# A two-layer hybrid attention encoder step: five places in the hand-written order of its engines

## What is computed

```python
z = x @ W_in                    # four head groups and a gate of width 2048
# A: forgetting attention, 4 heads   B: chunk band with relative bias, 4 heads
# C: sliding window, 4 query and 2 kv heads, rotary, sinks
# D: attention into 256 memory tokens, 4 heads, keys and values = mem @ W_mem_kv
y = (concat(heads) * silu(gate)) @ W_out
x = LayerNorm(ALPHA * x + y)
```

## Time and profile before

| | |
|---|---|
| median of the timed runs | 1963.86 us (1961.84 to 1964.38) |
| the profiled execution | 1964.82 us, span 1962.9 us, mean granted clock 0.994 |
| busy | PE 1914.5 us (98%), DVE 1395.5 (71%), ACT 872.5 (44%), POOL 153.6 (8%) |
| chain that ended last | PE 89%, DVE 3%, DMA 3%, ACT 2% |

### The profile page before, as it was taken

One profiled execution on the slowest core, in us unless ns is written; L12 is line 12 of the kernel. 1 busy time (PEld: TensorE's weight loads), 2 busy tenths in 40 slices (PEclk: granted clock), 3 DMA queues, 4 the chain that ended last, 5 costly groups with the idle time before them and its releaser, 6 DMA issues.

```text
span 1962.9 us, 37789 instructions
## 1 busy us (share of the span) xinstructions
PE 1914.5 (98%) x15232; PEld 1888.9 (96%) x15232; DVE 1395.5 (71%) x2435; ACT 872.5 (44%) x1557; POOL 153.6 (8%) x280
## 2 busy tenths in 40 slices
PE   7999999999999999999999999999999999999996
PEld 6999999999999999999999999999999999989996
DVE  6976676666677674777888666666677667657776
ACT  6543333333444444544574333333344444444444
POOL 0011010000000001000001000000000000100000
PEclk9999999999999999999999999999999999999998
DMA  8533333333222224555664323323323222335563
GB/s 302 210 108 108 118 121 101 121 121 121 100 94 98 102 90 176 192 206 195 224 224 142 117 97 106 110 103 115 114 94 119 76 88 104 126 136 205 192 216 144
DMA packets 71622, 271.70 MB, mean 138 GB/s; under 512 B 10108, under 2 KB 19964, under 8 KB 59664
## 3 DMA queue, kind: packets, MB, share of 16 engines
q1 hardware_dynamic: 44720, 202.13, 29.4%
q0 software_dynamic: 16320, 53.21, 7.6%
q10 hardware_dynamic: 10432, 14.29, 2.0%
HBM read 236.71 MB, written 35.50 MB: 139 GB/s over the span
## 4 chain that ended last, share of the span: by engine, by line
PE 89%; DVE 3%; DMA 3%; ACT 2%; issue 1%; POOL 0%; SPq 0%; ACTq 0%; DVEq 0%
PE GB L702 54%; PE GB L613 16%; PE GB L559 3%; PE AB L642 3%; PE AB L684 3%; PE GB L936 3%; DMA WR<-in_wt 2%; PE AB L653 2%; PE GB L574 1%; ACT S L1026 1%; DMA o_rest<-BD 1%; ACT WH L997 1%; DVE WL L1509 1%; PE AB L689 0%; DVE XL L2092 0%
## 5 line engine op out<-in xcount | busy, mean ns | idle before, releaser
L702 PE MATMUL GB<-XH,WH 128*128 128x272 f32 x2112 | 614.8, 291 | 0.0
L702 PE MATMUL GB<-XH,WL 128*128 128x272 f32 x2112 | 608.9, 288 | 0.0
L702 PE MATMUL GB<-XL,WH 128*128 128x272 f32 x2112 | 608.8, 288 | 0.0
L1069 ACT CAST WH<-WR 128x512 fp32r<-128x512 f32 (+1 forms) x336 | 249.1, 743 | 433.8 <-PE GB L702 219.9
L702 PEld LDWEIGHTS GB<-XH,WH 128*128 128x128 f32 x2112 | 398.3, 189 | 1.9
L702 PEld LDWEIGHTS GB<-XH,WL 128*128 128x128 f32 x2112 | 398.3, 189 | 0.0
L702 PEld LDWEIGHTS GB<-XL,WH 128*128 128x128 f32 x2112 | 397.3, 188 | 0.0
L1653 DVE TENSOR_TENSOR WL<-WR,WH 128x512 fp32r<-128x512 f32 (+1 forms) x336 | 281.2, 838 | 64.1 <-ACT WH L1069 59.8
L997 ACT CAST WH<-WR 128x2048 fp32r<-128x2048 f32 x88 | 167.9, 1908 | 207.5 <-PE GB L613 149.5
L1509 DVE TENSOR_TENSOR WL<-WR,WH 128x2048 fp32r<-128x2048 f32 x88 | 201.6, 2290 | 52.7 <-ACT WH L997 52.4
L702 PE MATMUL GB<-TH,WH 128*128 128x272 f32 x576 | 166.6, 289 | 0.0
(11 more groups left out here) (280 smaller groups left out, 2891.6 us busy)
## 6 DMA issues: line engine op xcount, KB each, us to landing
WR<-in_wt SPq DMA_DIRECT2D x192, 512.0 KB, 4.1
WR<-in_wt SPq DMA_DIRECT2D x88, 1024.0 KB, 4.8
XR<-out POOLq DMA_DIRECT2D x64, 136.0 KB, 2.8
out<-OY ACTq DMA_DIRECT2D x24, 272.0 KB, 2.2
OY<-o_rest POOLq DMA_DIRECT2D x2, 2992.0 KB, 14.4
out<-OY ACTq DMA_DIRECT2D x8, 544.0 KB, 5.0
out<-KT POOLq DMA_DIRECT2D x16, 272.0 KB, 3.5
out<-VT POOLq DMA_DIRECT2D x16, 272.0 KB, 3.6
```

Of the source, the lines that this page charges most:

```text
L702: mm = pe.matmul(out, w[:, k, :], x[:, k, :], start=(start and k == 0 and i == 0), stop=(stop and k == chunks - 1 and i == 2))
L1069: act.copy(weight_block(name)[0], weight_source(p, name)).then_inc(b_hi, 1)
```

## The change

It edits five places. (1) `DVE_PLAN[0]`: ("mv", 7) goes ahead of ("w", 6). (2) Late heads on ACT: `scale_probs` moves ahead of d1, and in d and e ahead of `mem_key`. (3) Pair b: the scores move from behind p7 to behind p6 (the hook name changes with the place). (4) `last_head`: `exps(MEM, u + 3)` goes ahead of the waits for `zh` and `ld_o`, all eight casts follow it, and DVE's `invert_sums` goes ahead of all `o_lo`. (5) `first_out_tiles`: chunk 15 of s = 0 runs between the second and third pass of s = 1, and the mean goes ahead of chunk 15 of s = 1.

```diff
@@ DVE_PLAN[0]
-     ("w", 6), ("mv", 7), ("w", 7), ("tokens", 0)],
+     ("mv", 7), ("w", 6), ("w", 7), ("tokens", 0)],
@@ first_out_tiles
+                def last_chunk(s):
+                    for i, (w, x) in passes:
+                        mm = part(s, [KC - 1], i, w, x, False, i == 2)
+                    mm.then_inc(zd, 1)
...
+                        if s == 1 and i == 2:
+                            last_chunk(0)
                         part(s, range(KC - 1), i, w, x, i == 0, False)
                     if s == 0:
                         between()
-                for s in range(2):
-                    for i, (w, x) in passes:
-                        mm = part(s, [KC - 1], i, w, x, False, i == 2)
-                    mm.then_inc(zd, 1)
                 mean()
+                last_chunk(1)
@@ two_tiles (TensorE); late_head asks for "p6" in pair b
                 sum_product("p7", "s3", 1)
-                hook("p7")
                 pe.wait_ge(c_copy, copied(p, "p1"))
                 sum_product("p6", "s2", 2)
+                hook("p6")
@@ late_head (ScalarE), pair a
                     exps(MEM, u - 1)
-                next_blocks(a, "d1")
-                if j:
                     scale_probs(MEM, u - 1, t - 1)
-                next_blocks(a, "a12")
+                next_blocks(a, "d1", "a12")
@@ pair d
                 exps(SWA, u + 1)
+                scale_probs(SWA, u + 1, t + 1)
                 mem_key(u + 2, kl + 1, dm)
                 if j == 0:
                     next_blocks(d, "d1")
-                scale_probs(SWA, u + 1, t + 1)
@@ pair e
                 exps(MEM, u + 2)
+                scale_probs(MEM, u + 2, t + 2)
                 mem_key(u + 3, kl + 2, dm + 1)
-                next_blocks(e, "d1")
-                scale_probs(MEM, u + 2, t + 2)
-                next_blocks(e, "a12")
+                next_blocks(e, "d1", "a12")
@@ last_head (ScalarE)
                 take_o(u + 2, KC - 2)
+                exps(MEM, u + 3)
                 act.wait_ge(zh, l + 1)
                 act.wait_ge(ld_o, 32 * (l + 1))
-                for c in range(4):
-                    o_hi(c, 0)
-                exps(MEM, u + 3)
-                for c in range(4, 8):
+                for c in range(8):
                     o_hi(c, 0)
                 scale_probs(MEM, u + 3, t + 3)
@@ last_head (VectorE)
                 soft_in(MEM, u + 3)
-                for c in range(8):
-                    o_lo(c, 0, l)
                 invert_sums(u + 3)
-                for c in range(8, KC - 1):
+                for c in range(KC - 1):
                     o_lo(c, 0, l)
```

More of the change, by code:

```diff
@@ L823, in late_head @@
                     mix(MEM, u - 1, kl - 1, dm=dm - 1)
-                two_tiles(l, late_pair(l, j, 1), {"p7": lambda: late_scores(SWA, l, u, kl, q)})
+                two_tiles(l, late_pair(l, j, 1), {"p6": lambda: late_scores(SWA, l, u, kl, q)})
                 two_tiles(l, late_pair(l, j, 2), {"p2": own_probs, "p5": lambda: mix(SWA, u, kl, vu)})
```

## The result

The changed kernel takes 1942.57 us, the median of four runs (1940.90 to 1943.88), beside 1964.12 for four runs of the kernel before (1961.84 to 1966.39): ratio 0.989, 95% interval 0.9873 to 0.9907. The profiled execution took 1940.90 us (span 1939.0, mean granted clock 0.996), 23.9 less than that of before. The forecast was 1941.0, range 1937.5 to 1949.5.

A forecast was written before the change was run, and what follows sets the result against it. PE is busy 98% of the span, so only its waits and clock falls can go: 10.4 + 0.7 + 2.05 + 2.95 + 3.0 + 1.2 + 3.0 = 23.3 us off 1964.82 gives 1941.5, taken as 1941.0; range 1937.5 to 1949.5.

The forecast's parts named there:

- Edit 2, 10.4 us: Late heads: scaling probabilities earlier on ACT removes six waits of PE's transposes, 10.4 us over both layers.
- cover of `mix`: Pair d: DVE's copies of transposed probabilities end about 1.5 us before PE reaches `mix`.
- rival B: Late heads: the wait moves from transposes to `mix`, losing about half the scaling gain; 1946 us, chance 0.11.
- rival D: Late heads: ACT holds d1 and key casts behind scaling that waits for a late reciprocal; slower, 1989 us, chance 0.03.
- Edit 3, 0.7: Pair b, j = 0, layer 0: p6's matmuls cover the scores' wait, gaining 0.7 us; nothing taken as lost elsewhere.
- Edit 4, 2.05 and 2.95: Last head: earlier exponentials bring chunk 8's cast forward, ending PE's pass 2.05 us earlier in layer 0, 2.95 in layer 1.
- Edit 5, 1.5 a layer: First output tiles: the next tile's weight cast and low part come in time, gaining 1.5 us a layer, 3.0 in all.
- rival C: Output stage: low parts, sums and weight loads bind it and 3 us return; 1944 us, chance 0.09.
- Edit 1, 1.2: Before the first head: an earlier memory tile lets the first scores start 1.2 us earlier, though PE's 2.0 us wait goes.
- The cap: First scores cannot start before 111.7 us, when DVE's low query part is ready, however early PE is.
- The clock, 3.0: Layer 1: two falls of PE's clock, 1.5 us each, go with the removed waits; likely, not certain.

The follow-up runs named there:

- edit 2 alone: Kernel before with only the scaling of probabilities moved ahead of d1 and the key casts in pairs a, d, e: 1953.81 us, ratio 0.9941.
- edit 1 alone: Kernel before with only the turned memory tile moved ahead of w 6 in DVE's plan: 1965.32 us, ratio 1.000.
- ACT half of edit 4: Kernel before with only the last head's exponentials moved ahead of the casts on ACT, DVE's order unchanged: 1961.13 us, one run.
- edit 5 alone: Kernel before with only the first output tiles' chunk 15 and mean reordered: 1961.13 us, ratio 0.998.
- edit 4 alone: Kernel before with only the last head reordered, exponentials ahead of casts on ACT and reciprocal ahead of low parts on DVE: 1957.34 us, ratio 0.996.
- kernel without edit 3: Changed kernel with the scores of pair b put back behind p7: 1946.07 us, one run.

## Why the prediction was right

**Edit 2, 10.4 us.** 10.0 by the medians with and without it, 10.7 by the heads of two profiles without a fall. The waits went whole and arrived at the end of the stage. The cover of `mix`, which I put at 1.5 us, is 607.72 - 606.35 = 1.4; rival B stayed away because of it, and for rival D: d1's cast starts 2.65 us behind the reciprocal, where it was 2.0 before, 0.65 later of the 0.9 that I had counted, and nobody waits for it.

**Edit 3, 0.7.** The mechanism held (no wait in pair b), nothing was given back; the size was that of one execution. The 0.25 us of layer 1 were not in the forecast.

**Edit 4, 2.05 and 2.95.** 2.04 and 2.84. Chunk 8 was the right place to look, and ACT's pace of one chunk in 0.32 us up to chunk 14 the right limit behind it.

**Edit 5, 1.5 a layer.** 1.39 and 1.32 at the first tiles and up to 0.4 behind. Of rival C little is shown: the changed kernel waits for a weight's low part in layer 0's output stage for 0.2 us in one profile and 0.7 in the next. But three kernels without edit 5 wait there too (0.29 us with edit 2 alone, 0.40 with edit 1 alone, 0.31 with the ACT half of edit 4), and edit 5 alone does not.

**Edit 1, 1.2.** The cap was right: scores at 112.02, where I had said 111.7 at the earliest, and a wait of 2.12 where I had said 0.8 or 2.4. What failed is the step that took 1.2 us as this edit's gain. I measured it from 112.91, and PE is at 112.91 only because the clock fell at 85. I had seen that PE is slowed there ("or 2.4 if it is not slowed before"), and did not ask what the kernel before does in an execution that is not: its scores stand at the same cap. The edit by itself gives 1.000, and 38.03 us from forget gates to scores, as without it.

**The clock, 3.0.** In the profiles 4.2 us of falls went, these 3.0 and the 1.2 above. But the falls differ from one execution to the next, and the new wait of the first scores can bring one too: of the six profiles in which it is 1.5 us or longer, three have a fall there, and of waits of 2.12, 2.15 and 2.20 us only the second. The medians give 21.6 us where the two first profiles give 23.9; that fits about one fall more in the timed runs of the changed kernel than in its profile, but these runs have no trace to count them in. That the forecast is within 1.6 us of the median rests partly on chance. Its waits came to 19.1 us, and the two profiles without their falls differ by 19.7. Its falls came to 4.2 (3.0 and, unknown to me, the 1.2 of edit 1), which is the draw of one profile; the medians leave 1.9 for them (21.6 - 19.7, an estimate). The Trainium skill (TensorE: Matmul & The Clock Gate, What's actually happening) says that the clock follows how busy PE has recently been. The traces agree in that each fall stands in or behind a wait of PE of 1.0 us or more (one began inside the wait of 4.53 us, the others 0.4 to 2.5 us behind the end of theirs), and none came where the waits were gone. That does not tell which wait brings one: edit 4 alone kept six waits of up to 1.6 us and had no fall at them.

Shown by runs: that edits 2, 4 and 5 gain and by which waits, that edit 1 gains nothing in its stage, that the DVE half of edit 4 carries 0.9 us, that the scores' wait follows the load. Not settled: why one execution has a fall behind a given wait and another has none. No run here held the wait and changed something else to find out.

## What to carry to other kernels

When an engine takes its work in order, put what the bound engine waits for first and what it has slack for behind it, and check on both engines of the chain (here DVE's reciprocal as well as ACT's scaling): the ACT half of edit 4 alone left 0.9 of 2.0 and 2.8 us. A time read from one profile can hold a clock fall; compare a stage with the same stage in a kernel where that part is not changed before you call the difference a gain. Moving work ahead of a dependency that itself hangs on a late DMA only lengthens the wait there; issuing the load 20 us earlier was worth 2.0 us in that stage, where edit 1 was worth nothing.

## What the runs showed of the hardware

**One short wait can halve TensorE's clock for a while.** In and behind waits of 1.0 to 4.5 us there stood, in some executions, a fall to the 1.2 GHz level that cost about 1.5 us, or 2.9 where it was long (22.76 us for first output tiles that take 19.85). With the longest of these waits, 4.53 us, it was a long one, but so it was with one of 1.03 us. Edit 4 alone had six waits of 1.45 to 1.64 us in its late heads and no fall at them.

**Two-input operations on DVE and POOL's addition exclude each other.** The low part of the cached keys (L1621, 128x256) takes 0.42 us alone. In the kernel without edit 3 the late load moved it behind the start of POOL's addition for the bias:

```profile
108.31 1.42 POOL L2331 TENSOR_TENSOR BD<-BI,causal 128x512 f32<-128x512 f32 x1 [3.83 <-DMA BI<-nc_rows]
108.49 1.52 DVE L1621 TENSOR_TENSOR SPL<-KTC,SPL 128x256 fp32r<-128x256 f32 x1
```

It ends 0.28 us behind POOL's end (109.73). In the changed kernel the same happened to the weight's low part at 108.86, 1.77 us where the next of its shape took 0.73. And the other way round: POOL's addition took 1.28 us with edit 2 alone, where it began just before DVE's second low part of the token sums (107.32 and 107.35), and that low part took 2.40. In the changed kernel the low part began first (107.65), took 1.28, and the addition took 2.39:

```profile
107.69 2.39 POOL L2331 TENSOR_TENSOR BD<-BI,causal 128x512 f32<-128x512 f32 x1 [3.39 <-DMA BI<-nc_rows]
```

So DVE's chain and POOL's have lengths that depend on which of the two begins first. The Trainium skill (SBUF — State Buffer, SBUF: two separate sides) says that a DVE instruction with two inputs in SBUF and a POOL instruction that reads SBUF need the same pair of ports, and that whichever starts first holds it for its whole instruction while the other is blocked. The traces agree, by the 1.52 and 2.40 us on DVE and the 2.39 on POOL, each where the other engine had begun first.
